# A causal mask added by VectorE in the score bank, in place of a product of the identity with the mask

## The reference

```
s = jnp.einsum('bqhd,bkhd->bhqk', q_blk, k) * scale
s = s + c_q - c_k                      # cumulative log forget gate
s = jnp.where(k_pos <= q_pos, s, NEG_INF)
p = softmax(s);  out = p @ v
```

## Time and profile before

| | us |
|---|---|
| median of 3 runs | 1940.44 |
| the profiled execution's own time | 1940.12 |
| its span | 1938.4 |
| TensorE busy | 1880.6 |
| VectorE busy | 1407.4 |
| ScalarE busy | 709.8 |
| attention phase, layer 0 | from about 469 to 592 |
| attention phase, layer 1 | from about 1420 to 1543 |

### The profile page before, as it was taken

One profiled execution on the slowest core, in us unless ns is written; L12 is line 12 of the kernel. 1 busy time (PEld: TensorE's weight loads), 2 busy tenths in 40 slices (PEclk: granted clock), 3 DMA queues, 4 the chain that ended last, 5 costly groups with the idle time before them and its releaser, 6 DMA issues.

```text
span 1938.4 us, 24919 instructions
## 1 busy us (share of the span) xinstructions
PE 1880.6 (97%) x9113; PEld 1579.4 (81%) x9113; DVE 1407.4 (73%) x1997; ACT 709.8 (37%) x1070; POOL 335.8 (17%) x291
## 2 busy tenths in 40 slices
PE   7999999999999999999999999999999999999996
PEld 6888888889878888888888888888888888888884
DVE  6778777952566787787887777886446586778778
ACT  4232423334554324233233242333355442423321
POOL 5200000153314500000160000003343251000002
PEclk8999999999999999999999999999998999999998
DMA  5232223235732222222322222232557222222231
GB/s 221 74 116 92 108 87 130 95 118 179 210 96 88 104 92 108 87 108 87 131 87 109 87 108 87 108 114 101 175 159 202 71 93 87 108 87 108 87 130 43
DMA packets 41927, 217.07 MB, mean 112 GB/s; under 512 B 8724, under 2 KB 9172, under 8 KB 17928
## 3 DMA queue, kind: packets, MB, share of 16 engines
q1 hardware_dynamic: 38984, 200.35, 29.0%
q0 software_dynamic: 2880, 15.90, 3.5%
HBM read 198.28 MB, written 17.93 MB: 112 GB/s over the span
## 4 chain that ended last, share of the span: by engine, by line
PE 86%; DVE 6%; issue 2%; DMA 2%; ACT 2%; SPq 1%; POOL 1%; ACTq 0%; DVEq 0%; POOLq 0%
PE psum L949 79%; PE psum L1146 3%; DMA rawA<-in_a_w 2%; SPq L428 1%; DVE res L1410 1%; PE psum L1240 1%; PE psum L977 1%; DVE st L1434 1%; DVE negm L1742 1%; PE psum L1230 1%; DVE hl L1487 0%; ACT psum L873 0%; DVE xlo L1389 0%; PE psum L1340 0%; PE psum L1218 0%
## 5 line engine op out<-in xcount | busy, mean ns | idle before, releaser
L949 PE MATMUL psum<-xhi,whiA 128*128 128x512 f32 (+1 forms) x768 | 288.2, 375 | 10.3 <-DVE xlo L1389 10.3
L949 PE MATMUL psum<-whiD,hl 128*128 128x512 f32 x832 | 283.9, 391 | 3.6 <-DVE hl L1487 2.8
L949 PE MATMUL psum<-xlo,whiA 128*128 128x512 f32 (+1 forms) x768 | 286.6, 373 | 0.0
L949 PE MATMUL psum<-xhi,wloA 128*128 128x512 f32 (+1 forms) x768 | 286.5, 373 | 0.0
L949 PE MATMUL psum<-xhi,whiB 128*128 128x512 f32 x704 | 273.9, 389 | 0.0
L949 PE MATMUL psum<-xlo,whiB 128*128 128x512 f32 x704 | 273.9, 389 | 0.0
L949 PE MATMUL psum<-xhi,wloB 128*128 128x512 f32 x704 | 273.9, 389 | 0.0
L759 ACT ACTIVATE s<-psum 128x512 f32<-128x512 f32 x36 | 21.5, 598 | 576.3 <-PE psum L949 576.3
L1508 DVE SCALAR_TENSOR_TENSOR nat<-psum,nat 128x1024 f32<-128x1024 f32 x144 | 175.9, 1222 | 26.3 <-PE psum L949 26.3
L949 PEld LDWEIGHTS psum<-whiD,hl 128*128 128x128 f32 x832 | 156.2, 188 | 39.5 <-DVE hl L1487 4.5
L1508 DVE SCALAR_TENSOR_TENSOR res<-psum,res 128x1024 f32<-128x1024 f32 x108 | 132.0, 1222 | 76.1 <-PE psum L949 76.1
(11 more groups left out here) (205 smaller groups left out, 3586.7 us busy)
## 6 DMA issues: line engine op xcount, KB each, us to landing
rawA<-in_a_w SPq DMA_DIRECT2D x63, 1024.0 KB, 6.3
rawB<-in_b_w SPq DMA_DIRECT2D x54, 1024.0 KB, 4.7
rawD<-in_d_w SPq DMA_DIRECT2D x46, 1024.0 KB, 4.8
stacks<-hl SPq DMA_DIRECT2D x192, 64.0 KB, 1.8
whiD<-stacks POOLq DMA_DIRECT2D x10, 768.0 KB, 6.1
wloD<-stacks POOLq DMA_DIRECT2D x10, 768.0 KB, 5.7
gbr<-in_gb_row SPq DMA_DIRECT2D x7, 1024.0 KB, 8.3
stacks<-wloD SPq DMA_DIRECT2D x48, 64.0 KB, 1.7
```

The costliest lines, as they stand in the source:

```text
L949: ins = t_.matmul(out_, a_, b_, start=(start and k == 1), stop=(stop and k == n), skip_group_check=check)
```

## The change

`maskr` becomes a float32 tile, `identr` and its copy are gone. The product of line 1220 is removed from `scores`, and `s_done[m]` is signalled by the last score matmul. `row_max` first adds `maskr` to the last 128 columns of each map's bank in place, each add behind its `s_done[m]` and signalling a new semaphore `mask_ok[m]`, and then reduces each map behind `mask_ok[m]`. Both adds of a differential turn stand ahead of both reductions.

```
-        identr = sb("identr", [P, P], F32R)
-        maskr = sb("maskr", [P, P], F32R)
+        maskr = sb("maskr", [P, P])
...
+        mask_ok = [sem(f"mask_ok{m}") for m in range(2)]
...
-                            t_.matmul(bank[i][:, 0:n_], tile[0:STACK, n, t * P:t * P + P], tile[0:STACK, 2 + n, 0:n_],
-                                      start=(n == 0 or maps == 2), stop=False)
-                        t_.matmul(bank[i][:, t * P:n_], identr[:, :], maskr[:, :], start=False, stop=True).then_inc(s_done[m], 1)
+                            ins = t_.matmul(bank[i][:, 0:n_], tile[0:STACK, n, t * P:t * P + P], tile[0:STACK, 2 + n, 0:n_],
+                                            start=(n == 0 or maps == 2), stop=(n == 1 or maps == 2))
+                        ins.then_inc(s_done[m], 1)
...
-            v.tensor_copy(identr[:, :], ident[:, :])
...
-                    for m in range(2 if is_diff(G) else 1):
+                    maps = range(2 if is_diff(G) else 1)
+                    for m in maps:
+                        d = bank[2 * (G % 2) + m][:, w_ - P:w_]
+                        dve.wait_ge(s_done[m], count(l, G, m))
+                        v.tensor_tensor(d, d, maskr[:, :], ALU.add).then_inc(mask_ok[m], 1)
+                    for m in maps:
                         i = 2 * (G % 2) + m
-                        dve.wait_ge(s_done[m], count(l, G, m))
+                        dve.wait_ge(mask_ok[m], count(l, G, m))
                         v.tensor_reduce(negm[:, i:i + 1], bank[i][:, 0:w_], AX.X, ALU.max,
                                         negate=True).then_inc(max_ok[m], 1)
```

## The result

| | time, us | ratio to before, 95% interval |
|---|---|---|
| before | 1940.5 | |
| after, first measurement | 1955.4 (1953.0 to 1957.0) | 1.0076 [1.0061, 1.0091] |
| after, measured again (a13) | 1952.2 (1951.2 to 1956.1) | 1.0065 [1.0053, 1.0077] |
| forecast | 1948.0 (1943.5 to 1953.5) | |

The change makes the kernel slower, by 14.7 us in the first measurement and 12.6 in the second (ratio less one, times 1940.5). The forecast was +7.7: the sign was right, the size was not, and the part of the loss that was missed lies in a place that was forecast to gain.

The account below looks back on a forecast made before the run. It took the VectorE-ScalarE loop to bound the differential bodies and a weight-tile transfer chain the fox bodies' first halves. Differential +9.0, fox -1.2, body 4 zero and start -0.1 gave +7.7 us: 1948 us, range 1943.5 to 1953.5.

Parts of the forecast that it names:

- What bounds the kernel: Differential bodies 1 and 3: the VectorE-ScalarE loop, not TensorE, is late; in fox bodies 0 and 2, the weight-tile transfer chain.
- What goes: TensorE's queue: each of 112 removed mask products costs 0.11 to 0.12 us, 12.9 us at most.
- What comes: VectorE's adds: 0.21 us each in a row, 0.42 a differential pair, about 0.33 where the next instruction waits.
- The 0.26 us estimated beside it: The Trainium skill's estimate for one VectorE add from PSUM, making a pair 0.52 and the total 1950.4 us; not adopted.
- Differential bodies: Bodies 1 and 3: adds lengthen the loop; +2.5 and +2.5 in layer 0, +2.9 and +1.1 in layer 1, together +9.0 us.
- Body 4: Last fox body: two adds on the chain, +0.66 us, against six removed products, -0.69; zero.
- Start: Kernel start: the identity's copy leaves VectorE's queue ahead of the first input halves, -0.1 us.
- Fox bodies: Bodies 0 and 2: five products saved, 0.6 us, against one add's delay, +0.3; -0.3 per body, -1.2 in all.
- Rival C: Added idle time halves TensorE's clock in the four differential bodies: +6 us, 1954 us; chance 0.10.
- The range: Whole kernel: 1943.5 to 1953.5 us, from pairs of 0.30 to 0.66 us making paid turns 6.9 to 15.

Follow-up runs that it names:

- e1: The changed kernel without its adds, so no mask is applied and the products are gone too: 1936.6 us, ratio 0.9983 to the kernel before.
- e9: The changed kernel with each add right ahead of its own reduction, in place of both adds first: 1959.0 us, ratio 1.0102 to the kernel before.
- e2: The kernel before with the add put in besides the mask product in every turn: 1952.2 us, ratio 1.0060 to the kernel before.
- e4: The kernel before with the add in the fox turns alone, the product kept in the differential turns: 1942.4 us, ratio 1.0011.
- b12: The kernel before with eight idle 512-column products ahead of TensorE's wait for the key in body 3: 1939.6 us, ratio 0.9982.
- f2: The changed kernel with the mask product kept in body 0's eight turns in both layers, the add everywhere else: 1947.5 us, ratio 1.0028 to the kernel before.
- f3: The changed kernel with an idle 128-column product behind the scores of each of body 0's eight turns: 1945.9 us, ratio 1.0021 to the kernel before.
- e6: The changed kernel with ten idle 128x512 products ahead of turn 6's value products in body 0: 1950.0 us, ratio 1.0045 to the kernel before.
- f1: The kernel before with the add in place of the product in body 0's eight turns alone, both layers: 1941.6 us, ratio 1.0007.
- e11: The kernel before with the add in fox turns alone, plus ten idle products ahead of turn 6's value products in body 0: 1941.7 us, ratio 1.0014.
- e8: The changed kernel with the differential turns' mix one turn later in VectorE's queue: 1975.9 us, ratio 1.0180 to the kernel before.

## Why the prediction was wrong

- **What bounds the kernel.** Right: the loop of VectorE and ScalarE bounds the differential bodies, not TensorE (e1: -3.3 us and not -8 or more).
- **What goes.** 0.115 us a product: right (0.11).
- **What comes.** 0.21 in a row, 0.42 a pair: right (0.20, 0.40). The 0.33 for an exposed add: right (e9). The 0.26 us estimated beside it is neither the duration measured (0.292) nor the distance (0.20); the 1950.4 that it led to is nearer to the result, but by luck.
- **Differential bodies.** Body 1 +2.5 and +2.9: +2.4 and +2.8, the same within 0.1 in every kernel that adds there in this order. Body 3 +2.5 and +1.1: +3.1 and +1.3 (2.3 to 3.2 and 1.2 to 1.7 in the others). In layer 1 TensorE's clock is 0.50 there as before, and the room it gives was counted rightly. +9.0 forecast, +9.6 measured. In layer 0 the clock falls at the start of body 3 too, which the prediction did not see, and for a time that differs from profile to profile; before, after and a13:

```profile
540.00:550.00 10.00, 8.67 (x51) 7.84 (x50) 7.69 (x19) 5.01 (x15) 2.76 (x3) 0.83 0.59 170
544.00:554.00 10.00, 9.13 (x34) 7.56 (x33) 7.63 (x23) 4.19 (x13) 1.40 (x3) 0.52 0.56 168
544.00:554.00 10.00, 8.76 (x47) 7.81 (x47) 8.11 (x24) 4.30 (x14) 2.39 (x3) 0.83 0.58 177
```

With 0.52 the body gave +3.1, with 0.83 +2.3. The wait of 1.90 us ahead of it is the same in all three.
- **Body 4.** 0: +0.3 a layer. The wait of the earlier trace rows grew from 0.64 to 1.34, by 0.70 where two adds were put at 0.66; e2 has +0.7 there and e1 -0.5, so what fell short is the products' 0.69.
- **Start.** -0.1: -0.6 at turn 0 of layer 0. This is scatter as far as is known: profiles of kernels whose start is unchanged lie between -1.3 (e4) and +0.4 (b12) there.
- **Fox bodies: "Net -0.3 for each of four bodies".** This is the step that failed, in body 0: +2.2 and +3.4. Body 2 gave -1.1 and -0.8, in the second profile -0.2 and +1.4. The two layers' +5.6 against -0.6 are 6.2 us, more than the 5.2 by which the span missed the forecast. I counted the instructions that go and come on the path, with the transfer's duration as a constant ("No mask product lies on that stretch"). The runs show that it goes with TensorE's pace in the turns before. By turn 4 TensorE is 0.44 us early, the transfer lasts 1.8 us longer (7.00 against 5.21), TensorE stands for 2.8 us, and runs on at a lower clock. f2 and f3 show the missing products, and not the adds, as the cause of body 0's loss in the changed kernel: with the products kept there it is back at 0 and -0.2, with idle products in their place at -0.9 and -0.3, and the whole is at 1947.5 and 1945.9, 0.5 and 2.1 us under the forecast.
- **Rival C** named a mechanism that is at work, TensorE's clock behind idle time, and looked for it in the wrong place: it fell in body 0, behind waits of 2.8 us, and not in body 1, whose waits of 0.25 to 0.69 us left it at 1.00. Nor was layer 1 "the one place" where it fell before: in layer 0 it is 0.59 over 541 to 545. The Trainium skill, "TensorE: Matmul & The Clock Gate", section "What's actually happening", says that idleness halves the clock and activity restores it; e6 and b12 agree, as far as an idle product is activity: filled, both stretches keep 1.00.
- **The range.** By its own terms the low end was too high: with the pair at 0.30, body 1 gives 1.7 and 2.1, body 3 1.8 and 0.4, so 6.0 and not 6.9. It changes nothing in the outcome.

**What stays open.** Why the transfer takes 7 to 9 us in place of 5 to 6: the next body's stack load and the query's puts share its time, and a faster pace moves the puts towards it, but the distance alone does not order the profiles (in before 3.5 us lie between its issue and the puts and it takes 5.6; in f1 4.0 in both layers, and it takes 8.2 in layer 0 and 5.2 in layer 1). And why layer 1's body 0 loses mostly where the differential turns add too (after, a13, e6 and e9; not e1, e4, e11, f1, and not e8): this is the part that is not additive in e1 to e4, and no run took it apart. To the same part belongs f1, where the faster pace of body 0 in a kernel otherwise as before costs nothing that can be measured (1.0007). The slower pace was made with work in every case; a pause of the same length without work was not tried.

## What to carry to other kernels

An instruction that is moved from a full engine to one with 27% idle time costs all that it puts between its neighbours (here 0.20 us each, not its 0.29 of duration) where the second engine stands in a loop with others: read the spacing of one loop turn, not the busy shares. Where a stage waits for a transfer that other transfers run beside, its duration belongs to the pace around it; making the engine ahead faster by 0.1 us a turn may cost microseconds, so put such a stage's own range into the forecast, and test it with idle work of the removed size. A wait of two to three microseconds on TensorE can cost twice, by its length and by the clock behind it, and idle products ahead of it can bring the second part back (e6: 4 to 6 us).

## What was not expected of the hardware

- Sixteen idle products of 128 columns made the changed kernel 8.5 us faster.
- Two dependent VectorE instructions are 0.33 us apart where independent ones of the same duration, 0.29, are 0.20 apart (e9 against the changed kernel).
- TensorE's waits of 0.25 to 0.69 us in body 1 left its granted clock at 1.00. The changed kernel's waits of 2.5 to 3 us in body 0 were followed by a fall (0.57 over 486 to 490), and so was one of 2.04 us in e1; but one of 2.74 us in e4 was not (1.00 over 484 to 488), nor one of 2.47 us in a13, body 2 of layer 1 (1.00 over 1494 to 1500). The length of one wait does not settle it.
